# Eight half-width reloads of the expert rows, later matrix loads ahead of them, and six edits to who works when

## What is computed

```
for i in range(2):                                   # first block
    u = rmsnorm(x, g_mix[i]) @ w_in[i]
    y_a = stick_breaking_attention(...)  @ w_br_a    # 8 heads
    y_b = differential_attention(...)    @ w_br_b    # 4 heads, each head normed
    x = x + (sigmoid(gate_a) * y_a + sigmoid(gate_b) * y_b) @ w_o[i]
    h = rmsnorm(x, g_ffn[i])
    x = x + hierarchical_moe(h, ...)                 # 32 experts, the best 2 per token
    ple_gate = sigmoid(rmsnorm(x, g_ple[i]) @ w_ple_gate[i])
    x = x + (p[i] @ w_ple[i]) * ple_gate
x = rmsnorm(x, g_final)
f1 = swiglu(rms_norm(x, ffn1_pre_g), ...)            # second block
x = x + 0.5 * rms_norm(f1, ffn1_post_g)
x = x + rms_norm(hybrid_mixer(rms_norm(x, mix_pre_g), ...), mix_post_g)
f2 = swiglu(rms_norm(x, ffn2_pre_g), ...)
x = x + 0.5 * rms_norm(f2, ffn2_post_g)
```

## Time and profile before

| what | value |
|---|---|
| median of 3 runs | 3189.02 us (3187.94 to 3191.88) |
| profiled execution: its own time | 3188.17 us |
| profiled execution: span of the trace | 3186.4 us |
| mean granted TensorE clock (1 is 2.4 GHz) | 0.974 |
| PE busy | 3005.5 us, 94% |
| DVE, ACT, POOL busy | 42%, 19%, 26% |
| memory read, whole span | 513.41 MB |

### The profile page before, as it was taken

The page is one execution under the profiler, slowest core; times in us unless marked ns, Lnnn a source line. Parts: engine busy times, 40 slices in busy tenths (PEclk is TensorE's granted clock), DMA queues, the critical chain, the costliest instruction groups (busy, mean ns, idle before and its releaser), DMA issues. The chain is left out here.

```text
span 3186.4 us, 31434 instructions
## 1 busy us (share of the span) xinstructions
PE 3005.5 (94%) x12384; PEld 1872.5 (59%) x12384; DVE 1327.9 (42%) x2188; ACT 619.5 (19%) x1009; POOL 829.0 (26%) x637
## 2 busy tenths in 40 slices
PE   8999998999899999989997999998999999799996
PEld 6854464333368544643333688885754345588885
DVE  5346443111343565431223644424344464544442
ACT  2032322111210333221112300002012341300000
POOL 5200022232132000122221154444300001345443
PEclk9999999999899999999998999998999999899998
DMA  4211123999522111149996122221211111122220
GB/s 181 80 53 40 53 84 128 386 386 392 214 79 80 53 40 53 66 142 370 379 378 248 67 92 89 84 93 66 93 72 40 66 40 53 62 85 93 80 93 27
DMA packets 80915, 412.75 MB, mean 130 GB/s; under 512 B 25793, under 2 KB 25921, under 8 KB 34177
## 3 DMA queue, kind: packets, MB, share of 16 engines
q1 hardware_dynamic: 56144, 387.67, 31.9%
q0 software_dynamic: 24624, 23.08, 2.2%
HBM read 513.41 MB, written 31.46 MB: 171 GB/s over the span
## 5 line engine op out<-in xcount | busy, mean ns | idle before, releaser
L2708 POOL TENSOR_TENSOR ATT<-ring 128x512 f32<-128x512 f32 (+1 forms) x95 | 122.2, 1286 | 1199.0 <-PE PS L966 730.5
L966 PE MATMUL PS<-G,ring 128*128 128x256 f32 x1312 | 310.3, 379 | 0.0
L966 PE MATMUL PS<-HT,ring 128*128 128x256 f32 x1216 | 282.4, 385 | 21.1 <-ACT HT L2260 15.3
L966 PE MATMUL PS<-G,ATT 128*128 128x256 f32 x1184 | 280.8, 380 | 0.0
L966 PEld LDWEIGHTS PS<-G,ring 128*128 128x128 f32 x1312 | 249.3, 190 | 33.9
L966 PEld LDWEIGHTS PS<-HT,ring 128*128 128x128 f32 x1216 | 233.7, 193 | 59.9 <-issue 15.2
L966 PEld LDWEIGHTS PS<-G,ATT 128*128 128x128 f32 x1184 | 225.7, 191 | 32.7 <-issue 2.0
L2448 ACT ACTIVATE TMP<-PS 128x256 f32<-128x256 f32 x89 | 34.2, 384 | 1067.5 <-PE PS L966 947.9
L909 PE MATMUL PS<-ring,G 128*64 128x512 f32 x1024 | 228.5, 599 | 2.5 <-ACT G L2420 2.5
L523 PE MATMUL PS<-HT,ring 128*128 128x512 f32 x448 | 205.4, 601 | 3.9 <-DVE G L1412 3.9
L1865 DVE TENSOR_TENSOR BIG<-PS,TMP 128x256 f32<-128x256 f32 x100 | 42.4, 424 | 357.1 <-ACT TMP L2448 355.2
(11 more groups left out here) (340 smaller groups left out, 4475.1 us busy)
## 6 DMA issues: line engine op xcount, KB each, us to landing
ring<-in_stream SPq DMA_DIRECT2D x164, 1024.0 KB, 4.8
ring<-in_experts_gu SPq DMA_DIRECT2D x128, 1024.0 KB, 8.7
ring<-in_experts_down SPq DMA_DIRECT2D x64, 1024.0 KB, 8.8
G<-expert_rows SPq DMA_DIRECT2D x8, 1024.0 KB, 7.8
h_tokens<-G POOLq DMA_DIRECT2D x2, 2048.0 KB, 7.4
XT<-in_xT SPq DMA_DIRECT2D x2, 1024.0 KB, 8.1
G<-in_pT POOLq DMA_DIRECT2D x2, 512.0 KB, 6.4
out_T<-XT SPq DMA_DIRECT2D x2, 512.0 KB, 3.6
```

What stands on the lines that cost most here:

```text
L966: mm = pe.matmul(product(g, name), x[:, k * P:(k + 1) * P], y[:, k, :], start=first and k == 0 and name in ("P1", "P2", "P3", "P5"), stop= ...
L2708: pool.tensor_tensor(a["S1"], a["A21"], a["A22"], ALU.add)\
```

## The change

1. **Rows reloaded in eight parts.** SP first issues the four loads of the per-layer gate's weights, then waits for the scattered rows, then reloads them in 8 transfers of 512 KB, first the lower 512 features of all tokens and then the upper. DVE adds and PE turns half by half. Each transfer now consists of 2 KB pieces where it had 8 KB ones.
2. **First unit interleaved** (`two_tiles`, `first_unit`): for each HT tile both products at once. The norm's sum moves behind it. At the mixer's start the third tile goes to PSUM bank 5, so the norm's sum can come after its third product.
3. **Ranks** by 5 products: one of 128 columns, then four that each count one block of tokens for all later ones at once (128, 96, 64, 32 columns).
4. **Sigmoids of 8 gates on ACT alone**: exp, ln(1 + x), exp of the negative; they run after the attention's weights instead of before them. DVE's add and reciprocal are gone.
5. **Head norms** come before the last tile of the first branch on DVE.
6. **The second feed-forward's first unit** becomes plain and tile by tile, POOL forms no sums for it, and the norm's sum moves into the unit behind.
7. **Zeroing** of the lower part of BIG moves from POOL to ACT.

The core of the diff:

```diff
+            def two_tiles(block, banks, rhs):
+
+                for k in range(KD):
+                    pe.wait_ge(Q["raw_ready"], now.next("raw_ready"))
+                    mm = [pe.matmul(banks[m], block(m, k), rhs[:, k, :], start=k == 0, stop=k == KD - 1)
+                          for m in range(2)]
+                return mm
+
+            def first_unit():
...
+                for mm in two_tiles(lambda m, k: w[:, k, m * P:(m + 1) * P], banks, HT):
+                    mm.then_inc(Q["lin_ready"], now.inc("lin_ready"))
+                unit_used("lin_ready")
...
-                for t in range(TT):
-                    for s in range(t + 1):
-                        mm = pe.matmul(PS[:, 5, t * NE:(t + 1) * NE], BEFORE if s == t else ONES, M[:, s, :],
-                                       start=first, stop=s == t, skip_group_check=True)
-                        first = False
-                for t in range(TT):
-                    mm = pe.matmul(PS[:, 5, TT * NE:(TT + 1) * NE], ONES, M[:, t, :],
+                pe.matmul(PS[:, 5, 0:TT * NE], BEFORE, ATT[:, 0:TT * NE], start=True, stop=False, skip_group_check=True)
+                for t in range(TT):
+                    mm = pe.matmul(PS[:, 5, (t + 1) * NE:(TT + 1) * NE].rearrange("p (t x) -> p t x", x=NE), ONES,
+                                   M[:, t, :].unsqueeze(1).to_broadcast([P, TT - t, NE]),
...
-                for t in range(TT):
-                    pe.wait_ge(Q["comb_ready"], now.next("comb_ready"))
-                    for f in range(KD):
+                for half in range(2):
+                    for t in (2, 3, 0, 1):
+                        pe.wait_ge(Q["comb_ready"], now.next("comb_ready"))
+                        for f in range(4 * half, 4 * half + 4):
...
+                    if f == 1 and i == 0:
+                        a = weight_blocks(w, u, 4)
+                        a = [[a["A11"], a["A12"]], [a["A21"], a["A22"]]]
+                        mm = two_tiles(lambda m, k: a[m][k // 4][:, k % 4 * P:(k % 4 + 1) * P], [PS[:, 0, :], PS[:, 1, :]],
+                                       HT)[-1]
...
-                        if i == 0 and name == "P5" and f == 1:
-                            norm_sum(KD, 7)
+                        if i == 1 and name == "P3" and f == 1:
+                            norm_sum(KD, 3)
...
+            first_unit()
+            w = unit()[:, 0:KD * P].rearrange("p (k c) -> p k c", k=KD)
+            for k in range(KD):
+                mm = pe.matmul(PS[:, 5, :], w[:, k, :], HT[:, k, :], start=k == 0, stop=k == KD - 1)
+                if k == 2:
+                    norm_sum(KD)
...
-                    if j:
-                        next_sigmoid()
                     rope([DAQ[:, j, :]], COS, SIN)
-                    if j:
-                        for k in range(SB_GATE[j - 1] + 1, SB_GATE[j]):
-                            next_sigmoid()
...
+                for t in (2, 3, 0, 1):
+                    combine(0, t)
+                begin_sum("x_ready")
+                for k, t in enumerate((2, 3, 0, 1)):
+                    combine(1, t)
+                    add_rows(k)
+                for k in range(TT, KD):
+                    add_rows(k)
...
                 sub_norm()
+                first_branch(HT, KD - 1, KD - 1)
...
+                act.activation(G[:, k, :], G[:, k, :], ACT.Exp, scale=-1.0).then_inc(Q["act_step"], now.inc("act_step"))
+                act.wait_ge(*now.prev())
+                act.activation(G[:, k, :], G[:, k, :], ACT.Ln, bias=1.0).then_inc(Q["act_step"], now.inc("act_step"))
                 act.wait_ge(*now.prev())
                 act.activation(G[:, k, :], G[:, k, :], ACT.Exp, scale=-1.0).then_inc(Q["g_exp"], now.inc("g_exp"))
...
+                    weights(2 * j)
+                    weights(2 * j + 1)
                     if j:
                         for k in range(SB_GATE[j - 1], SB_GATE[j]):
-                            g_exp(k, lin0 + order.index(("gate", k)) + 1)
-                    weights(2 * j)
-                    weights(2 * j + 1)
+                            sigmoid(k, lin0 + order.index(("gate", k)) + 1)
...
+                        for i in range(2):
+                            act.activation(BIGF[:, i * 4 * S:(i + 1) * 4 * S], ONES[:, 0:1].to_broadcast([P, 4 * S]),
+                                           ACT.Identity, scale=0.0).then_inc(Q["rx_zeroed"], now.inc("rx_zeroed"))
...
-                pool.memset(BIGF[:, 0:8 * S], 0.0).then_inc(Q["tails_zeroed"], now.inc("tails_zeroed"))
...
+                for _ in range(N_PLE_U):
+                    load()
 
                 for par in range(2):
                     sp.wait_ge(Q[f"y_store{par}"], 16 * (L + 1) * NSEQ // 2)
-                for t in range(TT):
-                    sp.dma_start(YG[:, 2 * t:2 * t + 2, :].rearrange("p c d -> p (c d)"),
-                                 YDR[2 * t * P:2 * (t + 1) * P, :].rearrange("(p c) d -> p (c d)", c=2))\
-                        .then_inc(Q[f"y_gathered{t}"], 16)
-                for _ in range(N_PLE_U):
-                    load()
+                for half in range(2):
+                    for t in (2, 3, 0, 1):
+                        sp.dma_start(YG[:, 2 * t:2 * t + 2, half * 512:(half + 1) * 512],
+                                     YDR[2 * t * P:2 * (t + 1) * P, half * 512:(half + 1) * 512]
+                                     .rearrange("(p c) d -> p c d", c=2))\
+                            .then_inc(Q[f"y_got{half}{t}"], 16)
```

More of the change, by code:

```diff
@@ L547, in new_item, with sums_of @@
                 return u
+            def sums_of(u):
+                return u + 1 - ("ffn1" in at and u > at["ffn1"][0])
             def item_done(u):
@@ L1046, in _, with layer_sums @@
                 at[f"in{L}"] = (len(at["items"]), len(at["groups"]), t0)
[L1047 to L1061 removed]
+                first_unit()
+                def layer_sums(name):
+                    if name == "P3":
+                        if L == 0:
+                            pe.wait_ge(Q["x_landed"], X_LANDED)
+                        norm_sum(KD)
+                        token_sums()
+                quartered_unit(t0, 1, layer_sums)
                 drained("lin_ready")
@@ L1906, in ffn @@
                 for i in range(0, KF, 2):
-                    quarter_sums(g0 + i, GATED)
-                    by_rstd(GATED, "gate_scaled")
+                    if f == 1 and i == 0:
+                        v.wait_ge(Q["unit_done"], at["groups"][g0]["done"])
+                        for m in range(2):
+                            v.wait_ge(*now.prev())
+                            v.tensor_tensor(GATED[:, m * S:(m + 1) * S], PS[:, m, :], RSTD[:, :], ALU.mult)\
+                                .then_inc(Q["tile_done"], now.inc("tile_done"))
+                    else:
+                        quarter_sums(g0 + i, GATED)
+                        by_rstd(GATED, "gate_scaled")
                     hid = BIGF[:, i * S:(i + 2) * S]
@@ L1997, in _ @@
                 token_tiles(g, DAV)
-                st["sigmoid"] = 0
                 stick_breaking()
+                v.wait_ge(Q["g_exp"], now.next("g_exp", SB_GATE[-2]))
                 def head_done(h):
@@ L2013, in _ @@
                 at[f"heads{L}"] = now.count("lin_free")
-                for k in range(len(DA_BRANCH), KD):
+                for k in range(len(DA_BRANCH), KD - 1):
                     first_branch(HT, k, k)
@@ L2097, in _ @@
             rstd_wait()
-            store_scaled(CQ, 3)
+            store_scaled(CQ, 3, spare=2)
             store_scaled(CKV, 2)
@@ L2694, in weight_sums @@
                     item = at["items"][u]
+                    if u == at["ffn1"][0]:
+                        continue
                     w = []
```

115 lines of the change are left out of this document (50 added, 65 removed).

## The result

The changed kernel takes **3134.94 us** (median of 4 runs, 3134.08 to 3140.18), the kernel before 3188.48 us beside it (4 runs, 3187.33 to 3191.88): a ratio of 0.9834, 95% interval 0.9817 to 0.9851. The profiled execution is the one of 3134.08 us, with a span of 3132.2 us and a mean granted clock of 0.984 (before 3188.17, 3186.4 and 0.974).

A forecast was written before the change was run, and what follows sets the result against it. TensorE (PE), busy 94% of the span, was taken as the bound, with its waits and the 1.2 GHz clock behind them. Terms of 4.4, 11.8, 14.6, 5.0, 0, 8.0 and 10.4 sum to 54.2 us: forecast 3135, range 3122 to 3152.

The forecast's parts named there:

- Layer ends, +4.4: Expert rows' reload at both layer ends: halves and earlier gate weights win 1.5 us net plus 2.9 in layer 1.
- (b): Layer ends: 2 KB pieces move at 391 GB/s at best, so reloading takes 10.7 us, not 9.9; extra issues 0.2.
- (c): Layer ends: DVE's four additions came 2.48 us apart, 1 MB each at 423 GB/s, so transfers set the pace.
- (d): Layer 1's end: fourth transfer came 1.4 us late beside the gate weights' loads; loading those earlier makes the gain 2.9.
- Sigmoids, 11.8: Stick-breaking attention: without DVE's reciprocals PE's 8.6 us of gate waits go, and 1.6 us of slow clock per layer.
- Head norms, 14.6: Head norms: scalings put ahead remove a 4.2 us wait and 3.1 us of slow stretch per layer, twice 7.3.
- Ranks, 5.0: Rank stage: 10 PE records remain of 28, saving 2.5 us twice, only if DVE is not late next.
- Mixer 8.0 and last feed-forward 10.4: First units there: using each HT tile once made fills PE's waits, winning 8.0 and 10.4 us.
- the slow stretches stay: Rival, chance 0.10: shorter pauses remain and the clock still falls at four places, 15 us back, 3150.
- the clock gives it back: Rival, chance 0.03: 1.2 GHz spells in long units; gain gone at 108 us of them, 3198 at mean clock 0.935.
- DVE is late for the layer end's sum: Rival, chance 0.12: POOL's sums slow DVE's norm at layer ends, up to 3.5 + 1.5 us per layer back, 3145.
- small transfers don't overlap: Rival, chance 0.03: each of eight reload transfers costs its full 3.6 us, last landing after 28.8, time 3167.

The follow-up runs named there:

- run 5: Kernel before, with only the last first branch of the gate taken after the four head-norm scalings: 3172.00 us against 3186.58, ratio 0.9953.
- run 6: Kernel before, with only the gate's sigmoids moved to ACT alone, after the pair's attention weights: 3174.16 us against 3186.58, ratio 0.9960.
- run 9: Changed kernel with the mixer's first unit as before, one tile of output after the other: 3146.76 us, ratio 0.9870 to the kernel before.
- run 10: Changed kernel with the last feed-forward's first unit as before, wanting four HT tiles to start: 3146.68 us, ratio 0.9872 to the kernel before.
- run 4: Changed kernel, with the next layer's loads issued only after the last row transfer has landed: 3143.19 us, ratio 0.9855 to the kernel before.
- run 8: Changed kernel with three 1 MB row transfers, the last in two halves, gate's weights loaded behind: 3133.76 us, ratio 0.9836 to the kernel before.
- run 7: Changed kernel with the expert rows' buffer zeroed by POOL's memset again, not by ACT: 3144.54 us, ratio 0.9872 to the kernel before.

## Why the prediction was right, and where not

**The bound.** Right: what paid was mostly a wait of TensorE taken away, with the slow clock behind it. Runs 5, 6, 9 and 10 each bear one term alone.

**Layer ends, +4.4: failed**, and the step that failed is the price of the halves.

(a) *"The last piece is half"*: from its addition to the product 1.65 us in place of 4.2, right.

(b) *"4.2 MB then take 10.7 in place of 9.9 us, and eight issues in place of four leave 0.2 more"*: by this the last half lands 13.2 us after the first issue, and the gate's product starts after 14.9. It landed after 15.9 and 16.3, and the product started after 18.2 and 18.0. Of the 3.3 and 3.1 us that are missing, 2.7 and 3.1 are the landing. The rate was right for most single halves (1.3 us apart, 400 GB/s), but they don't keep it: from a first landing at 4.4 us even that rate throughout ends at 13.8, and in every layer end with eight halves some come 1.6 to 2.9 us behind the one before, also with no other load in flight (run 4). The issues take 5.26 us, 0.66 each, against 1.98 for four; that does not set the end, since the eighth is issued 11.3 us before it lands. Why single halves come late stays open.

(c) *"The transfers set the pace"*: nearly. I never summed DVE's work between the landings. With four sums into XT drawn in between the halves' additions, DVE needs 1.6 us a step for 1.3 us of transfer, and a half's addition takes 0.69 us, not 0.6. That puts the last addition 0.0 to 0.9 us behind its landing (0.6 and 0.0 in the changed kernel).

(d) The 1.4 us won back in layer 1, where the fourth transfer came late *"with the gate weights' loads in flight beside it"*: whole transfers have a late fourth in one layer or the other, with the loads behind and ahead. A single row of one execution was read as a cause. What makes it late stays open too.

On batching transfers, which the forecast had put as a rival: the Trainium skill ("DMA: Bandwidth & Descriptors", section Bandwidth) says to make them at least 1 MiB. The rule pointed the right way here. Eight halves don't serialize as the rival had it, with a last landing after 28.8 us and 3167 us, and they lose less than its estimate of 8 us over four wholes: the last landing is 1.8 to 4.1 us later than the 12.2 of whole transfers that come on time. Run 8, with one short piece at the end of long ones, has 62.1 us to the late sums against means of 63.4 and 64.0, which is within the spread of single executions.

**Sigmoids, 11.8:** 12.2 measured; an operation of 512 columns takes 0.63 us on ACT (taken: 0.7). **Head norms, 14.6:** 14.3, with the slow stretch gone as forecast. **Layer starts, 0:** run 6 shows 0.

**Ranks, 5.0:** 6.7 measured. The term counted PE's records alone, 2.5 us a layer, and in layer 0 PE's counting did get 2.8 us shorter (3.91 to 1.14). But the bound of that stretch is nearly shared with DVE: before, PE came to the slot table's product 0.85 us after DVE's chain. So the records alone are worth 0.7 per layer (run 7), and the other 2.8 and 2.5 us came with the zeroing that left POOL. The forecast had that rightly as a condition (*"this counts only if DVE is not late next"*), but not in the sum. With it TensorE still waits 1.4 us for DVE in layer 0, so DVE's chain now sets the stretch there. That 6.7 lies near 5.0 is in part luck.

**Mixer 8.0 and last feed-forward 10.4:** 7.9 and 10.4, by the same steps: the last feed-forward's first tile is used 0.14 us after it is made, and the wait ahead of the seventh tile is 1.04 us at the mixer and 0.42 at the feed-forward, where 0.6 and 0.95 were forecast.

**What the forecast lacked.** 2.1 us in the experts and 1.7 in the first feed-forward, of which the change touches nothing. Before, the clock fell there for a few microseconds (two rows of the kernel before):

```profile
1407.60:1414.40 6.80, 4.87 (x20) 1.90 (x20) 0.00 (x0) 2.90 (x3) 3.09 (x4) 0.80 0.60 191
1795.20:1802.00 6.80, 5.58 (x14) 3.62 (x15) 6.36 (x7) 2.83 (x4) 0.00 (x0) 0.75 0.00 0
```

At the same instructions of the first feed-forward the changed kernel (1761.10 us) has:

```profile
1761.10:1767.90 6.80, 5.52 (x22) 4.16 (x23) 6.36 (x7) 2.90 (x4) 0.00 (x0) 1.00 0.00 0
```

22 records in place of 14, behind the same pause of 1.98 us. Such short slow stretches lie behind a pause of PE, but the same pause doesn't always bring them. Runs 8 and 4 are alike in code up to the first layer end. At their first layer's start PE goes on behind a pause of 3.17 us in both, and 16 records take 3.72 and 6.77 us:

```profile
42.84 3.72 PE L990 MATMUL PS<-HT,ring 128*128 128x256 f32 x16 [3.17 <-DVE BIG L1351]
...
43.38 6.77 PE L988 MATMUL PS<-HT,ring 128*128 128x256 f32 x16 [3.17 <-DVE BIG L1349]
```

From 45 to 52 us the granted clock was 0.67 in run 4, 0.86 in the changed kernel's profile and 1.00 in run 8, and softmax attention began at 295.75, 293.49 and 292.15 us. A few such places would make the 6 us between the fastest and the slowest run of one kernel, though one profile per run can't show it. So the exact hit is luck: a term that was 5.6 us too high met 3.8 us of clock and 1.7 us at the ranks that nobody had summed. Without the 3.8 us, and with all else as measured, the time is some 3139.

**Rivals.** That the slow stretches stay, and that the clock gives it back: no, it is 0.984 in place of 0.974. (That rival's sum was off as well: 108 us at half the clock lower the mean over 3188 us by 0.017, to 0.957 and not to 0.94.) That DVE is late for the layer end's sum: a wait of 1.6 us in layer 1 alone, less than its 5 us. That small transfers don't overlap: not as priced, but this rival named the place that failed.

## What to carry to other kernels

Before cutting a transfer into smaller pieces, find out when the last piece lands, not how fast one piece moves: here halving won 2.5 us behind the last addition and lost 1.8 to 4.1 us ahead of it. Only the last piece gains from being short. Add up also what the consumer does per piece: if that is more than a piece takes to land, it falls behind. Where two engines are nearly equally late at one point, speeding up one gives next to nothing until the other is faster too. An operation that stands still on DVE beside a POOL memset can hold a whole chain; look for a small operation with an absurd duration, and ask who else is at work then. Never take a cause from one row of one execution: cut several executions at the same instructions, and see what they differ by where the kernels are the same.

## What the runs showed of the hardware

- A DVE operation on 128x4 takes 3.00 us during POOL's memset of 128x4096 and ends within 0.04 us of it, and it takes 0.17 us beside ACT writing the same buffer (run 7 and the changed kernel). ACT needs 3.69 us for that zeroing, the memset 3.53.
- Eight transfers of 512 KB in 2 KB pieces take SP's queue 5.26 us to issue (6.22 in the changed kernel's layer 1), four of 1 MB in 8 KB pieces 1.98 us. The same 4.2 MB land 14.0 to 16.3 us after the first issue as eight, and 12.2 us after it as four, or 13.6 to 13.8 when the fourth is late, which it was in one of the two layers of each of five executions.
- TensorE's clock is at 1.2 GHz for short stretches behind pauses, and not in the same places in two executions: behind 3.17 us at the first layer's start, 16 records took 6.77 us in run 4 and 3.72 in run 8. In the changed kernel's experts, with pauses of up to 2.1 us for DVE, it stayed at 2.4 GHz up to the layer end's wait, while behind a pause of 1.74 us at the ranks it did so in layer 0 and not in layer 1 (0.83 from 1353 to 1360 us).
